# A 31-tap convolution shared by four engines: its TensorE part two dense tiles later, and the taps dealt out anew

## The chip, the cores and the metric

The kernel runs on one core of a Trainium2 chip. The metric is the device time of one execution in microseconds. Three runs of the kernel before took 1447.33, 1449.21 and 1451.06 us; their median is 1449.21 us.

## The reference, cut to what matters

A small transformer of three layers on one sequence of 512 tokens with 1024 features, all in fp32. The third layer's mixer is a conformer convolution: a projection to twice the width, a gate, a depthwise causal convolution over 31 tokens, a layer norm, SiLU, and a projection back.

```
def conformer_conv(x, w_in, b_in, conv_w, conv_b, ln_g, ln_b, w_out, b_out):
    a, g = jnp.split(x @ w_in + b_in, 2, axis=-1)
    h = a * jax.nn.sigmoid(g)
    h = lax.conv_general_dilated(
        h, conv_w[:, None, :].astype(h.dtype), window_strides=(1,),
        padding=[(CONV_KERNEL - 1, 0)],
        dimension_numbers=("NWC", "WIO", "NWC"),
        feature_group_count=D_MODEL) + conv_b
    h = jax.nn.silu(layer_norm(h, ln_g, ln_b))
    return h @ w_out + b_out
...
            y = conformer_conv(h, a_w_in[j], a_b_in[j], a_conv_w[j], a_conv_b[j],
                               a_ln_g[j], a_ln_b[j], a_w_out[j], a_b_out[j])
...
        x = x + y
        x = x + squared_relu_mlp(rms_norm_2(x, mlp_norm[i]), mlp_w1[i], mlp_w2[i])
```

The other two layers (a pooling mixer and a windowed attention, each with a gated feed-forward part) are not touched by the change.

## The kernel before

Features lie on the partitions, tokens along the free dimension, so that an activation of 1024 x 512 is eight chunks of 128x512. Every weight matrix is cut into units of 128 output features (128x1024 weights). A unit passes through four slots: SyncE loads it into `raw`, ScalarE copies it into the fp32r high part `whi` (`split_hi`, line 1027), and somebody makes the low part `wlo`, which is `raw` minus `whi`. TensorE then runs a `chain`: eight tiles of three matmuls (high by high, high by low, low by high, lines 637 to 639), 24 matmuls of 128x512 into one of four banks `acc`.

The convolution stage is the phase `ain`: 16 units, two per chunk c, one for the value and one for its gate. I call the two chains of a chunk its dense tile. Per chunk c, these things happen.

- VectorE evicts both banks (`evict`, line 1799), ScalarE takes the sigmoid of one (`sigmoid`, line 1322), and VectorE multiplies them into `hc` (`gated`, line 1809), a ring of three buffers that also holds 30 zero columns in front.
- The 31 taps of the chunk are shared. TensorE takes the first `PE_TAPS[c]`: SyncE copies shifted windows of `hc` into `shifted` (`shift_hc`, one DMA for each of `SHIFTS[c]` groups of partitions, line 505), VectorE builds small diagonal matrices (`diagonals`, line 1771), and `convolve(c)` runs `ROUNDS[c]` rounds of `SHIFTS[c]` small matmuls side by side (line 914). A round covers as many taps as there are shifts.
- The next `POOL_TAPS[c]` are products made by ScalarE (`products`, line 1300, a ring `tapped` of nine buffers) and added up by GpSimd into `prod` (line 623).
- The rest are VectorE's own taps (`own_tap`, lines 1747 and 1750), each of which adds into a PSUM bank and waits for the one before. TensorE's sets add into the same bank and wait until the chunk's own taps are done. The last `LATE_TAPS[c]` (`late_tap`, line 1760) come after TensorE's sets, and VectorE alternates them with the next chunk's own taps.
- `collect(c)` (line 1793) adds the bank and `prod` into `hv`; for the last chunk, whose own taps lie in another bank, there is an addition more (line 1788). ScalarE squares it (`square`, line 1317) and TensorE sums `hv` and its square over the features (`statistics`, line 937) for the layer norm.

The order on TensorE is: the dense tile of chunk c, `convolve(c-1)`, `statistics(c-3)`. `convolve(5)` is held back until the dense tile of chunk 7 is done, and what is left of the sets and the statistics comes behind it. After that the layer norm and the next projection (`aout`) start.

The low parts of units 6 to 19 (16 and above belong to `aout`) are not VectorE's: `LOW_AT` names, for each, after which addition of GpSimd's chain it is dealt with. Those in `POOL_LOW` are subtracted by GpSimd (line 611). For the others ScalarE writes the negative of `whi` into `wlo` (`negate_high`, line 1309) and GpSimd issues a DMA that adds the weights from HBM onto it (line 605). Their order on ScalarE is written out by hand: the second split of iteration c waits until the dense tile of chunk c+1 is done, since it needs the slot.

SyncE's queue is in order as well: load of unit 2c+6, `shift_hc(c)`, load of unit 2c+7.

Of the kernel before, what the change touches and what calls it, by code (L numbers as in the profile page):

```python
# [30 lines left out]
T = 512  # L31
# [11 lines left out]
PE_TAPS = (6, 6, 8, 8, 12, 12, 20, 14)  # L43
SHIFTS = (2, 2, 4, 4, 4, 4, 4, 2)
# [6 lines left out]
GATE_AT = 8  # L51
STATS_AFTER = 2
COLLECT_AT = 3
R1_CHUNKS = (3, 4, 5, 6)
R1_AT = 3
# [12 lines left out]
POOL_LOW = (6, 7, 8, 9)  # L68
# [109 lines left out]
def build(nc, xT, vec_in, cst_in, w_in, out):  # L178
# [3 lines left out]
    with ExitStack() as ctx:  # L182
# [3 lines left out]
        def sem(name):  # L186
            return ctx.enter_context(nc.semaphore(name))
# [133 lines left out]
        late_steps = sem("late_steps")  # L321
# [21 lines left out]
        def v(name, e=0):  # L343
            return col(vec, VEC[name] + e)
# [4 lines left out]
        def own_taps(c):  # L349
            return range(PE_TAPS[c] + POOL_TAPS[c], TAPS - LATE_TAPS[c])  # L350

# [282 lines left out]
        def _(pe):  # L634
# [383 lines left out]
        def _(act):  # L1018
# [314 lines left out]
            for c in range(C):  # L1333
                act.wait_ge(hc_ready, c + 2)
                products(c, range(4 if c == C - 1 else 2))
                if 2 <= c < C - 1:
                    square(c - 2)
                if c == C - 1:
                    square(c - 2)
                if c + 1 == C - 1:  # L1340
                    products(c, range(2, GATE_PRODUCTS))
                    sigmoid(c + 1)
                    products(c, range(GATE_PRODUCTS, POOL_TAPS[c]))
                else:
                    products(c, range(4 if c == C - 1 else 2, POOL_TAPS[c]))
                if c < C - 2:
                    e = 2 * (c + AHEAD) - (c == 0)
                    split_hi(p.unit, 0, e)
                    sigmoid(c + 1)
                    if e in ADDED:  # L1350
                        negate_high(e)
                    for e in range(2 * (c + AHEAD) + (c > 0), min(2 * (c + AHEAD) + 2, 2 * C + 1)):
                        split_hi(p.unit, 0, e)
                        if e in ADDED:
                            negate_high(e)
                if c == C - 2:
                    split_hi(p.unit, 0, 17)
                    negate_high(17)
            square(C - 2)
            split_hi(p.unit, 0, 18)  # L1360
            negate_high(18)
            nc.scalar.activation(eps[:, 4:5], eps[:, 0:1], ACT.Sqrt)
# [20 lines left out]
        def _(dve):  # L1383
# [353 lines left out]
            def late_taps(c):  # L1737
                return range(TAPS - LATE_TAPS[c], TAPS)

# [12 lines left out]

            def late_tap(c, n, k):

                x, w, at = hc[:, c % HC, k:k + T], v("conv_w", c * TAPS + k), bank[6 + c % 2][:]
                if n == 0:
                    dve.wait_ge(conv_done, c + 1)
                else:
                    dve.wait_ge(late_steps, sum(LATE_TAPS[:c]) + n)
                V.scalar_tensor_tensor(at, x, w, at, op0=ALU.mult, op1=ALU.add).then_inc(late_steps, 1)  # L1760
# [21 lines left out]
            def collect(c):  # L1782

                part = prod[:, c % 2, :]
                dve.wait_ge(tapped_steps, sum(POOL_TAPS[:c + 1]) - c - 1)
                if c == APART:
                    dve.wait_ge(tap_steps, sum(len(own_taps(j)) for j in range(c + 1)))
                    V.tensor_tensor(hv[:, c, :], part, hv[:, c, :], ALU.add).then_inc(own_added, 1)
                    part = hv[:, c, :]
                    dve.wait_ge(own_added, 1)  # L1790
                dve.wait_ge(late_steps, sum(LATE_TAPS[:c + 1]))
                dve.wait_ge(conv_done, c + 1)
                V.tensor_tensor(hv[:, c, :], bank[6 + c % 2][:], part, ALU.add).then_inc(hv_ready, 1)
# [19 lines left out]
            for c in range(C):  # L1813
# [14 lines left out]
                if c < C - 1:  # L1828
                    gated(c)
                if c < C - 1:  # L1830
                    diagonals(c)

                own, late = own_taps(c), late_taps(c - 1) if c else []
                if c == HELD:
                    own = own[:len(own) - HELD_TAPS]
                if c == HELD + 1:
                    held = own_taps(HELD)
                    for n in range(len(held) - HELD_TAPS, len(held)):
                        own_tap(HELD, n, held[n])
                    evict(C - 1, 0)  # L1840
                rounds = max(len(own), LATE_START[c] + len(late))
                issued = [min(n, len(own)) + min(max(n - LATE_START[c], 0), len(late)) for n in range(rounds)]
                split_at = [next((n for n in range(rounds) if issued[n] >= m), rounds - 1) for m in (1, 5)]
                gate_at = next((n for n in range(rounds) if issued[n] >= GATE_AT), rounds - 1)
                for n in range(rounds):
                    for j in range(2):
                        if n == split_at[j] and c < C - 1 and (c or j) and 2 * c + j + AHEAD not in OTHER_LOW:
                            split_lo(p.unit, 0, 2 * c + j + AHEAD)
                    if n == gate_at and c < C - 2:
                        evict(c + 1, 0)  # L1850
                    if n == min(R1_AT, rounds - 1) and c in R1_CHUNKS:
                        invert_residual(R1_CHUNKS.index(c))
                    if n == COLLECT_AT and c == C - 1:
                        collect(C - 2)
                    if n < len(own):
                        own_tap(c, n, own[n])
                    if 0 <= n - LATE_START[c] < len(late):
                        late_tap(c - 1, n - LATE_START[c], late[n - LATE_START[c]])
# [3 lines left out]
                if 0 < c < C - 1:  # L1862
                    collect(c - 1)
# [135 lines left out]
```

## Time and profile before

| | |
|---|---|
| median of three runs | 1449.21 us |
| the profiled execution | 1448.2 us, of which the span is 1446.4 us |
| busy share: TensorE, VectorE, ScalarE, GpSimd | 99%, 63%, 42%, 16% |
| mean granted TensorE clock | 0.996 |
| convolution stage: first tile's inputs to last addition into `hv` | about 921 to 1042 us |
| DMA over the span | 144.95 MB, mean 100 GB/s |

Times in the rows below are microseconds from the span's start. PE is TensorE, PEld its weight loads, DVE VectorE, ACT ScalarE, POOL GpSimd, SP SyncE. A line of the order in time gives the start, the length from the first start to the last end of the merged instructions, engine, line, operation, what is written from what, and the number; what stands in brackets is idle time before it and what ended that. An fp32 matmul leaves two records, so six matmuls count as x12.

### The profile page before, as it was taken

What the parts mean: (1) busy time and instruction counts of PE and PEld (TensorE: products, weight loads), DVE (VectorE), ACT (ScalarE), POOL (GpSimd) and SP (SyncE); (2) the same over time, 40 slices, a digit from 0 to 9 for tenths busy, and PEclk for the clock granted to TensorE, in tenths of its full rate; (3) what the DMA queues carried; (4) which work ended last, traced back from release to release, by engine and by line L of the source; (5) the groups of instructions that cost most, each with busy time, mean ns of one, the idle gap of its engine ahead of it and who ended that gap; (6) DMA issues with size and microseconds to landing.
All of it is one profiled execution on the core that took longest, in us unless ns stands there. A gap on an engine that the chain in (4) does not pass through costs nothing. (4 is left out here: it accounts for less than half of the span.)

```text
span 1446.4 us, 19981 instructions
## 1 busy us (share of the span) xinstructions
PE 1431.5 (99%) x6878; PEld 1168.8 (81%) x6878; DVE 916.0 (63%) x1324; ACT 614.1 (42%) x914; POOL 226.5 (16%) x172
## 2 busy tenths in 40 slices
PE   8999999999999999999999999899999999999999
PEld 7788888888887898888888888667588888888887
DVE  7877773573655667767754756889888653544532
ACT  5544442342546665444422424667664321222210
POOL 7100000000302231000000003599711000000000
PEclk9999999999999999999999999999999999999999
DMA  5233233233431012332332232249813332332321
GB/s 191 88 102 102 89 101 115 74 101 91 122 102 60 30 60 88 102 102 87 101 117 73 98 101 89 90 111 214 217 45 102 116 102 88 101 102 88 102 95 51
DMA packets 49756, 144.95 MB, mean 100 GB/s; under 512 B 10016, under 2 KB 10784, under 8 KB 49696
## 3 DMA queue, kind: packets, MB, share of 16 engines
q1 hardware_dynamic: 47408, 137.34, 29.7%
q0 software_dynamic: 1440, 5.24, 2.0%
q10 hardware_dynamic: 848, 1.59, 0.3%
q8 instruction: 35, 0.57, 0.2%
q14 instruction: 25, 0.20, 0.0%
HBM read 135.14 MB, written 2.10 MB: 95 GB/s over the span
## 5 line engine op out<-in xcount | busy, mean ns | idle before, releaser
L637 PE MATMUL bank<-xh,whi 128*128 128x512 f32 x1184 | 464.8, 393 | 0.2
L639 PE MATMUL bank<-xh,wlo 128*128 128x512 f32 x1184 | 460.9, 389 | 0.0
L638 PE MATMUL bank<-xl,whi 128*128 128x512 f32 x1184 | 460.8, 389 | 0.0
L1027 ACT ACTIVATE whi<-raw 128x1024 fp32r<-128x1024 f32 x244 | 255.7, 1050 | 245.7 <-PE bank L639 239.0
L1392 DVE TENSOR_TENSOR wlo<-raw,whi 128x1024 fp32r<-128x1024 f32 x230 | 288.7, 1255 | 41.7 <-ACT whi L1027 33.6
L637 PEld LDWEIGHTS bank<-xh,whi 128*128 128x128 f32 x1184 | 222.2, 188 | 54.7 <-issue 6.0
L639 PEld LDWEIGHTS bank<-xh,wlo 128*128 128x128 f32 x1184 | 222.2, 188 | 46.7
L638 PEld LDWEIGHTS bank<-xl,whi 128*128 128x128 f32 x1184 | 222.3, 188 | 46.4 <-issue 1.0
L637 PE MATMUL bank<-ahi,whi 128*128 128x512 f32 x608 | 236.5, 389 | 0.0
L638 PE MATMUL bank<-alo,whi 128*128 128x512 f32 x608 | 236.5, 389 | 0.0
L639 PE MATMUL bank<-ahi,wlo 128*128 128x512 f32 x608 | 236.5, 389 | 0.0
L1413 DVE TENSOR_TENSOR res<-bank,res 128x512 f32 (+1 forms) x80 | 55.3, 691 | 200.9 <-PE bank L639 200.9
L582 POOL TENSOR_TENSOR ssum<-ssum,sq 128x512 f32<-128x512 f32 x32 | 48.7, 1521 | 719.8 <-ACT sq L1047 387.3
L1467 DVE SCALAR_TENSOR_TENSOR tmp<-u,vec,tmp 128x512 f32<-128x512 f32 x176 | 124.0, 747 | 29.6 <-ACT tmp L1089 29.3
L638 PEld LDWEIGHTS bank<-alo,whi 128*128 128x128 f32 x608 | 114.1, 188 | 23.8
L637 PEld LDWEIGHTS bank<-ahi,whi 128*128 128x128 f32 x608 | 114.1, 188 | 23.6
L639 PEld LDWEIGHTS bank<-ahi,wlo 128*128 128x128 f32 x608 | 114.1, 188 | 23.6
L1089 ACT ACTIVATE tmp<-u,vec 128x512 f32<-128x512 f32 x88 | 71.5, 814 | 121.6 <-DVE u L1460 121.5
L1460 DVE TENSOR_TENSOR u<-bank,rinv 128x512 f32<-128x512 f32 x88 | 59.5, 686 | 64.0 <-PE bank L639 64.0
L623 POOL TENSOR_TENSOR prod<-prod,tapped 128x512 f32<-128x512 f32 x56 | 78.6, 1404 | 6.5 <-ACT tapped L1300 0.4
L1111 ACT ACTIVATE ahi<-tmp 128x512 f32 (+1 forms) x32 | 20.2, 632 | 121.8 <-DVE tmp L1493 121.8
L1093 ACT ACTIVATE gate<-tmp 128x512 f32<-128x512 f32 x44 | 27.9, 633 | 98.4 <-DVE tmp L1467 98.4
(196 smaller groups left out, 1313.2 us busy)
## 6 DMA issues: line engine op xcount, KB each, us to landing
raw<-w_ffn_up SPq DMA_DIRECT2D x88, 512.0 KB, 3.3
raw<-w_ffn_down SPq DMA_DIRECT2D x32, 512.0 KB, 3.3
raw<-w_mlp_up SPq DMA_DIRECT2D x32, 512.0 KB, 3.3
raw<-w_mlp_down SPq DMA_DIRECT2D x32, 512.0 KB, 3.3
raw<-w_ain SPq DMA_DIRECT2D x16, 512.0 KB, 3.6
raw<-w_ffn_down SPq DMA_DIRECT2D x16, 384.0 KB, 3.1
raw<-w_qkv SPq DMA_DIRECT2D x12, 512.0 KB, 3.3
raw<-w_wo SPq DMA_DIRECT2D x8, 512.0 KB, 3.4
```

Of the source, the lines that this page charges most:

```text
L582: nc.gpsimd.tensor_tensor(ssum[:, which, :], ssum[:, which, :], x, ALU.add)\
L623: nc.gpsimd.tensor_tensor(prod[:, c % 2, :], a, tapped[:, (made + k) % PARTS, :], ALU.add)\
L637: nc.tensor.matmul(out_, hi, mh, start=first, stop=False)
L638: nc.tensor.matmul(out_, hi, ml, start=False, stop=False)
L639: return nc.tensor.matmul(out_, lo, mh, start=False, stop=last)
L1027: nc.scalar.activation(whi[:, s, 0:tiles * P], raw[:, s, 0:tiles * P], ACT.Copy)\
L1089: nc.scalar.activation(tmp[:, k, :], u[:, k, 2:2 + T], ACT.Identity, scale=col(vec, par + 2), bias=col(vec, par + 3))\
L1093: nc.scalar.activation(gate[:, b, :], tmp[:, 2 * b + 1, :], ACT.Silu)\
L1392: V.tensor_tensor(wlo[:, s, 0:tiles * P], raw[:, s, 0:tiles * P], whi[:, s, 0:tiles * P].bitcast(F32), ALU.subtract).then_inc(lo_done, 1)
L1413: V.tensor_tensor(row(res, c), acc[k][:], row(res, c), ALU.add).then_inc(acc_free, 1)
L1460: V.tensor_tensor(u[:, k, 2:2 + T], acc[k][:], rinv[:], ALU.mult).then_inc(acc_free, 1)
L1467: V.scalar_tensor_tensor(tmp[:, k, :], u[:, k, shift:shift + T], col(vec, par + 4 * j + shift), tmp[:, k, :], op0=ALU.mult, op1=ALU.add).t ...
```

## The change

- Every chunk's sets come two dense tiles later: TensorE's order is now the dense tile of chunk c, `convolve(c-2)`, `statistics(c-3)`, without a held chunk.
- All chunks but the last use sets of four shifts. `PE_TAPS` rises from 86 to 98 in all, `POOL_TAPS` falls from 72 to 58, VectorE's taps rise from 90 to 92. There are no late taps.
- VectorE's own taps of chunk c are split over two iterations: `OWN_AT_ONCE[c]` of them in iteration c, the others in iteration c+1, followed by the eviction of the next tile's first bank (`EVICT_AT`), `collect(c-2)` and the diagonals.
- Low parts 8 and 9 go from GpSimd's subtraction to the negation and the accumulating DMA, and the places of all of them are new. ScalarE's order is rewritten: `square(c-3)` comes first in iteration c, sigmoid and first split come between the products.

```diff
-PE_TAPS = (6, 6, 8, 8, 12, 12, 20, 14)
-SHIFTS = (2, 2, 4, 4, 4, 4, 4, 2)
+PE_TAPS = (12, 8, 8, 12, 12, 12, 20, 14)
+SHIFTS = (4, 4, 4, 4, 4, 4, 4, 2)
...
-STATS_AFTER = 2
-COLLECT_AT = 3
+STATS_AFTER = 3
+COLLECT_AT = 8
...
-POOL_TAPS = (11, 10, 10, 9, 9, 9, 8, 6)
-LATE_TAPS = (2, 8, 10, 12, 9, 0, 0, 0)
-HELD = C - 3
-HELD_TAPS = 7
-LATE_START = (2, 2, 2, 0, 0, 0, 0, 0)
+POOL_TAPS = (10, 9, 8, 8, 7, 7, 5, 4)
+OWN_AT_ONCE = (3, 4, 4, 2, 5, 7, 6)
+EVICT_AT = (3, 0, 0, 0, 0, 2, 1)
 PARTS = 9
-GATE_PRODUCTS = 6
+GATE_PRODUCTS = 5
 HC = 3
-LOW_AT = {6: (0, 7), 7: (0, 9), 8: (1, 5), 9: (1, 7), 10: (2, 5), 11: (2, 7), 12: (3, 5), 13: (3, 7), 14: (4, 5), 15: (4, 7), 16: (5, 6), 17: (7, 1), 18: (7, 3),
-          19: (7, 5)}
+LOW_AT = {6: (0, 6), 7: (0, 9), 8: (1, 1), 9: (1, 3), 10: (1, 6), 11: (2, 1), 12: (2, 5), 13: (3, 1), 14: (3, 5), 15: (4, 1),
+          16: (5, 3), 17: (6, 3), 18: (7, 3), 19: (7, 3)}
-POOL_LOW = (6, 7, 8, 9)
+POOL_LOW = (6, 7)
...
-                if 1 <= c <= HELD:
-                    convolve(c - 1)
-                if c == C - 1:
-                    convolve(HELD)
+                if c >= 2:
+                    convolve(c - 2)
                 if c >= 3:
                     statistics(c - 3)
...
             for c in range(C):
+                if c >= 3:
+                    square(c - 3)
                 act.wait_ge(hc_ready, c + 2)
...
+                products(c, range(2 if c == 0 else 0, min(GATE_PRODUCTS, POOL_TAPS[c])))
+                if c < C - 1:
                     sigmoid(c + 1)
...
+                if 1 <= c < C - 2:
+                    split_hi(p.unit, 0, 2 * (c + AHEAD))
+                    if 2 * (c + AHEAD) in ADDED:
+                        negate_high(2 * (c + AHEAD))
+                products(c, range(GATE_PRODUCTS, POOL_TAPS[c]))
+                if c == 0:
+                    split_hi(p.unit, 0, 2 * AHEAD)
+                if c < C - 3:
+                    split_hi(p.unit, 0, 2 * (c + AHEAD) + 1)
+                    if 2 * (c + AHEAD) + 1 in ADDED:
+                        negate_high(2 * (c + AHEAD) + 1)
...
+                gated(c)
+                if c == 0:
+                    split_lo(p.unit, 0, AHEAD + 1)
+                else:
+                    last = own_taps(c - 1)
+                    for n in range(OWN_AT_ONCE[c - 1], len(last)):
+                        own_tap(c - 1, n, last[n])
+                    if c == 1:
+                        diagonals(0)
+                    if EVICT_AT[c] == 0:
+                        evict(c + 1, 0)
+                    if c >= 2:
+                        collect(c - 2)
                     diagonals(c)
...
+                for n in range(OWN_AT_ONCE[c]):
+                    if n and n == EVICT_AT[c]:
                         evict(c + 1, 0)
+                    if c == 0 and n == 2:
+                        split_lo(p.unit, 0, AHEAD + 2)
+                        evict(1, 0)
+                    own_tap(c, n, own[n])
+                if c in R1_CHUNKS:
+                    invert_residual(R1_CHUNKS.index(c))
                 if c == C - 2:
                     gated(C - 1)
                     diagonals(C - 1)
```

## Rows read from the trace of the kernel before

**Rows 1.** The page's busy time and share of the span, with the instructions.
```profile
PE 1431.5 (99%) x6878; PEld 1168.8 (81%) x6878; DVE 916.0 (63%) x1324; ACT 614.1 (42%) x914; POOL 226.5 (16%) x172
```

**Rows 2.** Two stretches of the stage: length, busy by engine, granted clock, DMA, GB/s.
```profile
946.33:960.16 13.83, 13.83 (x62) 9.70 (x60) 9.63 (x14) 6.34 (x9) 13.26 (x9) 1.00 0.23 77
...
987.57:1001.81 14.24, 14.24 (x84) 9.87 (x81) 13.70 (x20) 10.12 (x15) 13.41 (x11) 1.00 0.98 234
```

**Rows 3.** TensorE's order in time at the end of the second dense tile.
```profile
941.01 5.39 PE L914 MATMUL bank<-shifted,dg 128*64 128x512 f32 x12 [5.94 <-DVE bank L1750]
946.33 0.50 PE L637 MATMUL bank<-xh,whi 128*128 128x512 f32 x1
```

**Rows 4.** Stretches as in rows 2, over the hole and behind it.
```profile
935.00:941.00 6.00, 0.07 (x1) 0.02 (x1) 5.82 (x9) 5.00 (x7) 5.43 (x5) 0.87 0.26 89
941.00:945.00 4.00, 3.99 (x10) 1.38 (x12) 3.86 (x4) 2.65 (x5) 4.00 (x3) 0.50 0.31 65
```

**Rows 5.** TensorE's order in time: sets, statistics, the next dense tile.
```profile
957.44 2.80 PE L914 MATMUL bank<-shifted,dg 128*64 128x512 f32 x12
...
971.29 1.92 PE L914 MATMUL bank<-shifted,dg 128*32 128x512 f32 x16
973.03 0.39 PE L937 MATMUL bank<-hv,ones 128*32 128x256 f32 x2
...
973.57 0.50 PE L637 MATMUL bank<-xh,whi 128*128 128x512 f32 x1
...
985.28 1.93 PE L914 MATMUL bank<-shifted,dg 128*32 128x512 f32 x16 [0.52 <-DMA shifted<-hc]
...
1024.58 2.78 PE L914 MATMUL bank<-shifted,dg 128*32 128x512 f32 x24
```

**Rows 6.** The chain that ended last, in the stage's tail: start, length.
```profile
1039.17 1.28 POOL prod L623
...
1041.20 0.70 DVE hv L1793
```

**Rows 7.** VectorE's order in time: diagonals, eviction, alternating taps, taps in a row.
```profile
929.47 0.56 DVE L1771 TENSOR_TENSOR dg<-pair_id,pair_w 128x384 f32<-128x384 f32 x1
...
940.77 0.69 DVE L1799 TENSOR_TENSOR bank<-bank,rinv 128x512 f32<-128x512 f32 x1
...
942.35 2.16 DVE L1771 TENSOR_TENSOR dg<-pair_id,pair_w 128x384 f32<-128x384 f32 x1
...
948.75 0.75 DVE L1750 SCALAR_TENSOR_TENSOR bank<-hc,vec,bank 128x512 f32<-128x512 f32 x1
949.41 0.75 DVE L1760 SCALAR_TENSOR_TENSOR bank<-hc,vec,bank 128x512 f32<-128x512 f32 x1
...
1032.88 5.50 DVE L1750 SCALAR_TENSOR_TENSOR bank<-hc,vec,bank 128x512 f32<-128x512 f32 x7
```

**Rows 8.** ScalarE's order in time: a split, its negation, two products.
```profile
986.70 1.06 ACT L1027 ACTIVATE whi<-raw 128x1024 fp32r<-128x1024 f32 x1
987.78 1.06 ACT L1309 ACTIVATE wlo<-whi 128x1024 fp32r<-128x1024 f32 x1
988.75 1.42 ACT L1300 ACTIVATE tapped<-hc,vec 128x512 f32<-128x512 f32 x2
```

**Rows 9.** GpSimd's order in time: four additions, an accumulating DMA, an addition.
```profile
952.89 5.59 POOL L623 TENSOR_TENSOR prod<-prod,tapped 128x512 f32<-128x512 f32 x4
...
1006.89 0.87 POOL L605 DMA_DIRECT2D wlo<-w_ain  x1
1007.50 1.60 POOL L623 TENSOR_TENSOR prod<-prod,tapped 128x512 f32<-128x512 f32 x1
```

**Rows 10.** Weight loads, median us to landing (from 973, from 987); ScalarE behind one.
```profile
raw<-w_ain SPq DMA_DIRECT2D x2, 512.0 KB, 10.6
...
raw<-w_ain SPq DMA_DIRECT2D x1, 512.0 KB, 12.6
...
1003.68 1.07 ACT L1027 ACTIVATE whi<-raw 128x1024 fp32r<-128x1024 f32 x1 [4.17 <-DMA raw<-w_ain]
```

More of the change, by code:

```diff
@@ L50 @@
 QUADRANT = P // 4
-GATE_AT = 8
-STATS_AFTER = 2
-COLLECT_AT = 3
+STATS_AFTER = 3
+COLLECT_AT = 8
 R1_CHUNKS = (3, 4, 5, 6)
-R1_AT = 3
 DIAGS = 2
-POOL_TAPS = (11, 10, 10, 9, 9, 9, 8, 6)
-LATE_TAPS = (2, 8, 10, 12, 9, 0, 0, 0)
-HELD = C - 3
-HELD_TAPS = 7
-LATE_START = (2, 2, 2, 0, 0, 0, 0, 0)
+POOL_TAPS = (10, 9, 8, 8, 7, 7, 5, 4)
+OWN_AT_ONCE = (3, 4, 4, 2, 5, 7, 6)
+EVICT_AT = (3, 0, 0, 0, 0, 2, 1)
 PARTS = 9
-GATE_PRODUCTS = 6
+GATE_PRODUCTS = 5
 HC = 3
-LOW_AT = {6: (0, 7), 7: (0, 9), 8: (1, 5), 9: (1, 7), 10: (2, 5), 11: (2, 7), 12: (3, 5), 13: (3, 7), 14: (4, 5), 15: (4, 7), 16: (5, 6), 17: (7, 1), 18: (7, 3),
-          19: (7, 5)}
+LOW_AT = {6: (0, 6), 7: (0, 9), 8: (1, 1), 9: (1, 3), 10: (1, 6), 11: (2, 1), 12: (2, 5), 13: (3, 1), 14: (3, 5), 15: (4, 1),
+          16: (5, 3), 17: (6, 3), 18: (7, 3), 19: (7, 3)}
 OTHER_LOW = tuple(LOW_AT)
-POOL_LOW = (6, 7, 8, 9)
+POOL_LOW = (6, 7)
 ADDED = tuple(e for e in LOW_AT if e not in POOL_LOW)
@@ L320, in build @@
         tap_steps = sem("tap_steps")
-        late_steps = sem("late_steps")
         own_added = sem("own_added")
@@ L349, in own_taps @@
         def own_taps(c):
-            return range(PE_TAPS[c] + POOL_TAPS[c], TAPS - LATE_TAPS[c])
+            return range(PE_TAPS[c] + POOL_TAPS[c], TAPS)
         def o_at(t, s):
@@ L1333, in _ @@
             for c in range(C):
+                if c >= 3:
+                    square(c - 3)
                 act.wait_ge(hc_ready, c + 2)
[L1335 to L1341, printed above, removed]
-                    sigmoid(c + 1)
[L1343 to L1355, printed above, removed]
+                if c == 0:
+                    products(c, range(2))
+                    split_hi(p.unit, 0, AHEAD + 2)
+                products(c, range(2 if c == 0 else 0, min(GATE_PRODUCTS, POOL_TAPS[c])))
+                if c < C - 1:
+                    sigmoid(c + 1)
+                if 1 <= c < C - 2:
[9 more added lines that the diff above has]
+                        negate_high(2 * (c + AHEAD) + 1)
                 if c == C - 2:
@@ L1358, in _ @@
                     negate_high(17)
-            square(C - 2)
+            square(C - 3)
             split_hi(p.unit, 0, 18)
             negate_high(18)
+            square(C - 2)
             nc.scalar.activation(eps[:, 4:5], eps[:, 0:1], ACT.Sqrt)
@@ L1735, in _ @@
             V.memset(hc[:, :, 0:TAPS - 1], 0.0).then_inc(hc_ready, 1)
-            def late_taps(c):
-                return range(TAPS - LATE_TAPS[c], TAPS)
             def own_tap(c, n, k):
@@ L1751, in own_tap @@
                                        op0=ALU.mult, op1=ALU.add).then_inc(tap_steps, 1)
[L1753 to L1760, printed above, removed]
             def diagonals(c):
@@ L1790, in collect @@
                     dve.wait_ge(own_added, 1)
-                dve.wait_ge(late_steps, sum(LATE_TAPS[:c + 1]))
                 dve.wait_ge(conv_done, c + 1)
@@ L1827, in _ @@
                     evict(0, 0)
-                if c < C - 1:
-                    gated(c)
-                if c < C - 1:
-                    diagonals(c)
[L1833 to L1849, printed above, removed]
-                        evict(c + 1, 0)
[L1851 to L1858, printed above, removed]
+                own = own_taps(c)
@@ new lines, in _ @@
+                if c == C - 1:
+                    collect(C - 3)
+                    for n, k in enumerate(own):
+                        if n == COLLECT_AT:
+                            collect(C - 2)
+                        own_tap(c, n, k)
+                    continue
+                gated(c)
+                if c == 0:
+                    split_lo(p.unit, 0, AHEAD + 1)
[9 more added lines that the diff above has]
+                        collect(c - 2)
+                    diagonals(c)
@@ L1861, in _ @@
                     diagonals(C - 1)
-                if 0 < c < C - 1:
-                    collect(c - 1)
             mean, mean_sq, var, safe, std = (rms[:, e * NBLK:(e + 1) * NBLK] for e in range(5))
```

## The prediction

> **What bounds the kernel now.** The page comes first: TensorE is busy for 99% of the span [rows 1]. So a microsecond counts only if TensorE waits less or more. The stretches of the convolution stage come next [rows 2]: between its holes TensorE is full, VectorE works 9.6 to 13.7 us of each tile's 14, and the DMA share climbs to 0.98. The order in time on TensorE shows the one large hole [rows 3]: after units 2 and 3 it stands until 941.01, for VectorE's last own tap of chunk 0. The granted clock over it and behind it [rows 4] is 0.87, then 0.50, which is the 1.2 GHz level: (1 - 0.87) x 6.0 / 0.5 = 1.6 us of the hole were already slow, so the clock fell about 4.4 us after TensorE stopped. The sets of chunk 0 then took 5.32 us (941.01 to 946.33 [rows 3]), where chunk 1's same three rounds took 2.72 (a stretch of 13.83 from 946.33 less 11.11 of dense work [rows 2, 3, 5]). From 946 the tiles follow each other, apart from 0.52 us for a shifted transfer in front of chunk 3's sets [rows 5], until the last dense unit ends at 1024.58 [rows 5]. I call that moment E. In the tail GpSimd's last sum ends at 1040.45 and VectorE's last addition into hv starts at 1041.20 [rows 6], 16.6 us after E.
>
> **The change, part by part.** First the durations.
> - TensorE: a tile of two dense units is 11.11 us (946.33 to 957.44 [rows 3, 5]); a round of sets 0.91 with two shifts (2.72 / 3, above) and 0.87 with four (971.29 to 973.03, two rounds [rows 5]); statistics 0.54 (973.03 to 973.57).
> - VectorE: taps in a row on one accumulator start every 0.79 ((5.50 - 0.75) / 6 [rows 7]); alternating between two accumulators they start every 0.66 (948.75, 949.41 [rows 7]). `gated`, an eviction and hc, takes 1.58 (940.77 to the diagonals at 942.35), counted as 1.5; a bare eviction or collect is 0.61 of that, as its 0.69 overlaps the next. The diagonals took 0.56 to 2.16 [rows 7], whatever their size; I take 1.3 to 1.7.
> - ScalarE: a split 1.08 to its negation, a negation 0.97 to the next product, two products 1.42, so 0.7 for one [rows 8]; a square on the same 128x512 at no more than a product, 0.6. GpSimd: 1.43 per addition ((5.59 - 1.30) / 3); an accumulating transfer holds the queue 0.61 and its next addition takes 1.60 instead of 1.30, so 0.9 [rows 9].
>
> *Sets.* Before E both kernels run chunks 0 to 4: 3+3+2+2+3 = 13 rounds, then 3+2+2+3+3 = 13. Twelve taps more cost TensorE nothing; six rounds at 0.91 become 0.87: -0.2. A shifted window of four pieces instead of two for chunks 0 and 1 is SP time and 0.5 MB each; the next weight load starts about 3 us later than before, ten microseconds before its split: nothing.
>
> *Two tiles later.* `convolve(0)` now follows units 4 and 5, whose low parts VectorE makes by about 934 (hc(0) ends just before 929.47 [rows 7]; a low part, 1024 elements wide, at twice an eviction's pace at most 1.6, two taps 1.6, a low part 1.6): the hole (-5.9), the slow sets (-2.6) and the wait for chunk 3's transfer (-0.5) go. With -0.2: -9.2.
>
> *VectorE.* It now has 92 taps for 90, all in series. Iteration 2 is gated 1.5, ten taps 7.8 (9 x 0.79 + 0.66), evict 0.6, collect 0.6, diagonals 1.6, four taps 3.0 = 15.1 us; the six iterations from 1 come to 12.7, 15.1, 14.7, 15.5, 15.3 and 12.8 = 86.1, against TensorE's 13.4 to 14.3 per tile. VectorE falls behind, but the sets ask only for taps finished one iteration earlier, so this alone stops nothing before E.
>
> *GpSimd and ScalarE.* GpSimd loses 14 additions (-20 us) and two low parts by subtraction (2 x 2.4), and gains two transfers (2 x 0.9): it no longer sets the tail. Low parts 8 and 9 cost ScalarE a negation each.
>
> *The new wait.* `square(c-3)` now stands at the head of iteration c, behind the second split and negation of iteration c-1, while TensorE asks for its statistics in the same tile c. The chain to it is: evict(c,0) 0.7, sigmoid 0.6, split and negation 2.1, GpSimd's accumulating transfer and the addition behind it 2.3, ScalarE's last product 0.6 (it waits for that addition), split and negation 2.1, square 0.6, and seven hand-overs of under 0.1: 9.4 us. It cannot start before the tile's first unit is done, and TensorE then has 5.55 + 1.74 = 7.3 us: at least 2.1 us of waiting at the two-round tiles, 3 and 4.
>  - At tile 3 VectorE is late too. From evict(1,1) at 935.1: `gated` 1.5, six taps 4.6, diagonals, evict, diagonals 3.6, four taps 3.0, `gated` 1.5, ten taps 7.8: evict(3,0) starts at 957.1, and square(0) ends 9.3 later at 966.4. TensorE is there at 935.03 + 11.11 + 2.61 + 11.11 + 1.74 = 961.6. A wait of 4.9.
>  - Unit 11's split also needs its load, issued behind the four pieces at 953.4. Such loads landed after 10.6 and 12.6 us [rows 10] once accumulating transfers ran beside them; with 10.6 the wait is 5.3.
>  - That passes the 4.4 us after which the clock fell before, so I add the 2.6 us that it cost then.
>  - Tile 4: 2.2. Tile 5 has three rounds and no GpSimd in the chain: split, negation and square 2.8 after the tile against 2.6, and a load landing 0.8 late: 1.1.
>  Together 5.3 + 2.6 + 2.2 + 1.1 = +11.2, and E moves by -9.2 + 11.2 = +2.0.
>
> *Tail.* From E: sets of chunk 5 2.6, diagonals(7) 2.0, collect(5) 0.6, eight taps 6.3, collect(6) 0.7, square 0.7: statistics(6) at E + 13.0, where TensorE stands 1.3 us; two rounds 1.8, sums by token 1.0, last round 0.95, hand-over: the last addition starts at E + 17.3, against 16.6: +0.7.
>
> Sum: +2.7 on the profiled execution's 1448.2 (span 1446.4 and 1.8 around it) = 1450.9. The median of the runs is 1.0 above that execution, so 1451.9.
>
> *A rule against a row.* The rows say that a tap which waits for the one before costs 0.13 us more than one that does not [rows 7]. The Trainium skill, "VectorE: DVE Perf Modes", section "The DRAIN you can't avoid", says that a semaphore between VectorE operations costs nothing extra. By that rule the sum would be about 4 us under before, as in the last rival.
>
> **The rivals.**
> - *Loads land late each time* (slower). The DMA share was 0.98 and ScalarE waited 4.17 us for such a load [rows 2, 10]. If the loads of units 11, 13 and 15 land after 12.6, each of tiles 3 and 5 waits 2 us longer: +4.0, and 1455.9; diagonals at 2.16 every time add up to 1.2. It decides from about 11.5 us on. Against it: two transfers spread over longer tiles.
> - *Square comes in time, VectorE sets the pace* (faster). If the trace's chain is shorter than I make it, no wait is left; then gated(7) starts at 935.1 + 86.1 = 1021.2 and the last addition 16.0 later, 1037.2 against 1041.20: -4.0, 1445.2, and 1443.5 with diagonals at the 0.56 of the first one. Against it: the 2.1 us floor needs none of the uncertain prices.
> - *Taps start every 0.66 even in series* (the rule above). The twenty taps in front of evict(3,0) save 2.6, the wait at tile 3 is 2.3 to 3.3, the clock stays up, the tail is 1 us shorter: -4.0, 1445.2. Against it: the series of seven in rows 7, 0.79 apart.
> - *The change does nothing that counts*: its own waits just fill the hole; that lies inside my forecast.
>
> **How the numbers follow.** A run can tell about 0.3%, 4.35 us, from no change: 1444.9 to 1453.6. Forecast 0.55 (0.46 inside, 0.09 slower, since its own range is 1448.4, with the clock kept and loads in time, to 1455); late loads 0.20 (0.18 slower, 0.02 inside); VectorE's pace 0.15 (0.08 faster, 0.07 inside); quick taps 0.10 (0.03 faster, 0.07 inside). In sum faster 0.11, same 0.62, slower 0.27. Range 1445 to 1457.
>
> **What the changed profile would show.** No hole at 935; TensorE's wait for VectorE's tap replaced by waits of the 128x256 statistics for sq: about 5, 2 and 1 us at tiles 3, 4, 5, and half clock behind the first. E near 1026.6, GpSimd idle in the tail, taps in series 0.79 apart. If statistics wait under 1 us the whole middle of the sum is wrong; if half clock does not show, 2.6 comes off; if a dense chain waits for a low part, I have missed a transfer.

## The result and the profile after

The changed kernel took 1452.52 us in the median of 16 runs (1450.36 to 1455.74), the kernel before 1448.11 in 16 runs beside it (1446.71 to 1451.06): a ratio of 1.0031, 95% interval 1.0023 to 1.0039, so 4.4 us slower. The forecast was 1451.9 with a range of 1445 to 1457, and +2.7 as the difference. A second measurement gave 1.0036 (1.0024 to 1.0048).

The profiled execution took 1450.36 us. Its page, busy time per engine:

```profile
span 1448.6 us, 19996 instructions
PE 1432.2 (99%) x6902; PEld 1170.2 (81%) x6902; DVE 917.5 (63%) x1326; ACT 608.3 (42%) x902; POOL 203.6 (14%) x158
```

Only GpSimd's time moved much, 226.5 to 203.6 us [rows 1], and the end did not follow it. TensorE's waits in the convolution stage, each line with the sum in us, the count and the longest:

```profile
PE bank L932 <- ACT sq L1310: 9.0, 4, 5.9
PE bank L951 <- DVE hv L1772: 0.2, 1, 0.2
```

The wait for VectorE's tap [rows 3] and the one for the shifted transfer [rows 5] are gone. In their place TensorE waits four times for ScalarE's squares: three times at tiles 3 to 5 and once, 0.69 us, in the tail. (The second line is the short wait at the end of the stage, which the kernel before has too.) Its order in time shows where:

```profile
945.08 2.78 PE L909 MATMUL bank<-shifted,dg 128*32 128x512 f32 x24
...
966.74 0.64 PE L932 MATMUL bank<-hv,ones 128*32 128x256 f32 x2 [5.90 <-ACT sq L1310]
...
967.75 0.80 PE L632 MATMUL bank<-xh,whi 128*128 128x512 f32 x1
...
984.20 0.64 PE L932 MATMUL bank<-hv,ones 128*32 128x256 f32 x2 [2.18 <-ACT sq L1310]
...
985.21 0.80 PE L632 MATMUL bank<-xh,whi 128*128 128x512 f32 x1
...
1000.37 0.41 PE L932 MATMUL bank<-hv,ones 128*32 128x256 f32 x2 [0.20 <-ACT sq L1310]
...
1026.32 2.78 PE L909 MATMUL bank<-shifted,dg 128*32 128x512 f32 x24
```

TensorE now goes from unit 3 into units 4 and 5 without a stop, and the sets of chunk 0 follow at 945.08 in 2.78 us and not in 5.39 [rows 3]. Then the statistics of tiles 3, 4 and 5 wait 5.90, 2.18 and 0.20 us. The last row is E, the end of the last dense unit. Stretches of the same kernel (length, busy time of each engine, granted clock, DMA share, GB/s):

```profile
961.00:963.00 2.00, 0.00 (x0) 0.00 (x0) 1.87 (x3) 0.72 (x1) 1.86 (x2) 1.00 1.00 272
964.00:965.00 1.00, 0.00 (x0) 0.00 (x0) 0.96 (x2) 0.99 (x1) 0.76 (x1) 0.50 1.06 262
...
970.00:971.00 1.00, 1.00 (x5) 0.78 (x4) 0.94 (x2) 0.72 (x1) 0.87 (x1) 0.79 0.97 202
...
984.00:985.00 1.00, 0.81 (x8) 0.23 (x8) 0.93 (x3) 1.00 (x3) 1.00 (x2) 0.54 0.95 175
...
987.00:988.00 1.00, 1.00 (x5) 0.73 (x4) 0.96 (x2) 0.52 (x1) 0.86 (x2) 0.76 0.76 121
```

The granted clock goes to its 1.2 GHz level twice: within the wait at tile 3 and, which the forecast did not have, at the end of the wait at tile 4. Each spell is paid for in the statistics (1.01 us from 966.74 to 967.75 and from 984.20 to 985.21, against 0.54 [rows 5]) and at the head of the dense tile. ScalarE's order in time ahead of the first wait:

```profile
956.89 0.73 ACT L1315 ACTIVATE gate<-tmp,vec 128x512 f32<-128x512 f32 x1 [0.18 <-DVE tmp L1778]
957.52 1.04 ACT L1020 ACTIVATE whi<-raw 128x1024 fp32r<-128x1024 f32 x1
958.60 1.06 ACT L1302 ACTIVATE wlo<-whi 128x1024 fp32r<-128x1024 f32 x1
959.56 1.32 ACT L1293 ACTIVATE tapped<-hc,vec 128x512 f32<-128x512 f32 x2
962.17 0.72 ACT L1293 ACTIVATE tapped<-hc,vec 128x512 f32<-128x512 f32 x1 [1.28 <-POOL prod L618]
963.93 1.06 ACT L1020 ACTIVATE whi<-raw 128x1024 fp32r<-128x1024 f32 x1 [1.04 <-DMA raw<-w_ain]
965.02 1.06 ACT L1302 ACTIVATE wlo<-whi 128x1024 fp32r<-128x1024 f32 x1
965.98 0.61 ACT L1310 ACTIVATE sq<-hv 128x512 f32<-128x512 f32 x1
```

Here is the chain that the forecast set up, link by link: sigmoid, split and negation, a product held by GpSimd, a split held by its load, a negation, the square. VectorE's order in time, for its pace and the tail:

```profile
923.08 3.30 DVE L1804 RECIPROCAL rinv<-rms 128x512 f32<-128x512 f32 x1
...
948.38 7.88 DVE L1739 SCALAR_TENSOR_TENSOR bank<-hc,vec,bank 128x512 f32<-128x512 f32 x10
956.17 0.68 DVE L1778 TENSOR_TENSOR tmp<-bank,rinv 128x512 f32<-128x512 f32 x1
956.77 0.68 DVE L1772 TENSOR_TENSOR hv<-bank,prod 128x512 f32<-128x512 f32 x1
957.37 0.41 DVE L1751 TENSOR_TENSOR dg<-pair_id,pair_w 128x256 f32<-128x256 f32 x1
...
1043.15 0.69 DVE L1772 TENSOR_TENSOR hv<-bank,hv 128x512 f32<-128x512 f32 x1 [0.32 <-PE bank L909]
```

The first row is a mark for lining up the two executions: the same operation started at 923.87 before, so this one runs 0.79 us ahead at the stage's start. With that, E moved by 1026.32 + 0.79 - 1024.58 = +2.5 us, and the last addition into hv by 1043.15 + 0.79 - 1041.20 = +2.7.

### The profile page after: what moved, and what is told of

Its sections match the earlier page's. It is cut to its first block, busy times and chain, and to the rows that moved or that the text cites. A ratio compares the mean times of both kernels' runs of the same rounds, so it can differ in the third digit from the quotient of the medians.

```text
span 1448.6 us, 19996 instructions
## 1 busy us (share of the span) xinstructions
PE 1432.2 (99%) x6902; PEld 1170.2 (81%) x6902; DVE 917.5 (63%) x1326; ACT 608.3 (42%) x902; POOL 203.6 (14%) x158
## 4 chain that ended last, share of the span: by engine, by line
PE 91%; POOL 4%; DVE 1%; issue 1%; DMA 1%; ACT 1%; SPq 0%; ACTq 0%; POOLq 0%; DVEq 0%
PE bank L632 29%; PE bank L633 28%; PE bank L634 28%; POOL prod L618 2%; PE bank L783 1%; PE bank L811 1%; POOL res L567 1%; PE bank L796 1%; POOL ssum L577 1%; PE bank L909 1%; DMA res<-xT 1%; PE bank L997 0%; PE bank L998 0%; DMA raw<-w_ain 0%; PE bank L1001 0%
## 5 line engine op out<-in xcount | busy, mean ns | idle before, releaser
L1739 DVE SCALAR_TENSOR_TENSOR bank<-hc,vec,bank 128x512 f32<-128x512 f32 x83 | 62.7, 755 | 2.8
```

What stands on the lines that cost most here:

```text
L1739: V.scalar_tensor_tensor(hv[:, c, :] if c == APART and n == len(own_taps(c)) - 1 else at, x, w, at, op0=ALU.mult, op1=ALU.add).then_inc(ta ...
```

## The experiments

All ran in three sessions of four, each with 14 to 29 runs of the kernel before beside them (medians 1448.35, 1448.00 and 1448.64 us). Since these medians differ by 0.6 us, I compare each kernel by its difference to the kernel before of its own session. "Kernel 2" is the kernel of experiment 2, and so on. The diffs are against the changed kernel unless another is named.

**1. The changed kernel once more.** No edit.

> The changed kernel once more, unchanged, as the measure for its neighbours on the same chip. All theories: about 1.003 of the kernel before. Its profile is of another execution, so it also tells how much the wait in front of the statistics of chunk 0 (5.90 us in the first profile) and the half clock behind it differ from one execution to the next.

Measured: 1453.26 us (1451.42 to 1455.24), ratio 1.0036 (1.0024 to 1.0048), +4.9. The wait at tile 3 was 8.06 us in this execution. Its rows on TensorE and on ScalarE:

```profile
968.89 0.64 PE L932 MATMUL bank<-hv,ones 128*32 128x256 f32 x2 [8.06 <-ACT sq L1310]
```
```profile
966.09 1.06 ACT L1020 ACTIVATE whi<-raw 128x1024 fp32r<-128x1024 f32 x1 [3.19 <-DMA raw<-w_ain]
```

The split of unit 11 waited 3.19 us for its load, not 1.04, and the whole chain behind it came 2.16 us later. What varies from one execution to the next is the landing of that load, not its issue: SyncE starts on these loads at 952.5 us here and at 952.7 in the first profile, and those issued between 950 and 966 us took a median of 14.2 us here and 11.2 there.

**2. The square earlier.** The square of chunk c-2 directly behind the sigmoid of tile c+1, ahead of the two splits.
```
             for c in range(C):
-                if c >= 3:
-                    square(c - 3)
...
                 if c < C - 1:
                     sigmoid(c + 1)
+                if 2 <= c < C - 1:
+                    square(c - 2)
```

> Only ScalarE's order differs: square(c-2) right behind sigmoid(c+1) in iteration c, before the splits, instead of at the head of the next iteration. Theory 1 (the squares come late, behind the second split and negation): the waits of 5.9, 2.2 and 0.2 us and the 1.7 us of half clock go, the last dense unit of the stage ends 9 to 10 us earlier; VectorE then sets the tail, and 5 to 7 us are left in the whole, so 1446 us, below the kernel before. Theory 2 (VectorE's 92 taps in series set the pace anyway): the waits change their name to VectorE and the time stays within 1.5 us of the changed kernel. Theory 3 (the transfers are late): the splits still wait for loads and a dense unit for its low part, and the time stays.

Measured: 1440.86 us (1440.64 to 1443.55), ratio 0.9956 (0.9942 to 0.9969): -7.5 to the kernel before, some 12 less than the changed kernel. TensorE's waits in the stage and the stretches of tiles 4 to 7:

```profile
PE bank L909 <- DMA shifted<-hc: 1.5, 1, 1.5
PE bank L932 <- ACT sq L1310: 1.2, 2, 1.0
```
```profile
961.00:974.50 13.50, 13.50 (x77) 9.70 (x73) 12.98 (x19) 9.15 (x13) 10.27 (x9) 1.00 1.03 276
974.50:988.00 13.50, 13.50 (x72) 9.65 (x76) 13.02 (x18) 10.80 (x15) 10.98 (x9) 1.00 0.92 196
```

The waits of tiles 3 to 5 and both half-clock spells are gone; TensorE is busy for all of each stretch at full clock. E lies at 1014.03, 12.3 us earlier; the last addition starts at 1033.55, 9.6 earlier; most of the difference is that chunk 7's set now waits 1.51 us for its shifted copies and the statistics ahead of it 0.99 us for their square. ScalarE's split of unit 11 still waited 1.67 us for its load there, and it did no harm: nothing that TensorE needs at once stood behind it.

**3. The statistics later.** The square stays where the change put it; TensorE asks for it a tile later.
```
-                if c >= 3:
-                    statistics(c - 3)
+                if c >= 4:
+                    statistics(c - 4)
             convolve(C - 2)
+            statistics(C - 4)
```

> Only TensorE's order differs: the statistics one dense tile later (statistics(c-4) in tile c), the squares where the change put them. Theory 1: the same gain as with the early square, 5 to 7 us, since nobody asks for the square in its own tile any more, though ScalarE's chain is as long as before. Theory 2 and 3: no gain. If this gains and the early square doesn't (or the other way round), the chain in front of the square is not what I think.

Measured: 1441.32 us (1441.15 to 1442.86), ratio 0.9954 (0.9941 to 0.9968), -7.0. This is the same gain from the other end of the same dependence: what cost time was that square and statistics stood in one tile with two splits between, neither place by itself.

**4. TensorE kept busy in the wait.** 20 matmuls whose results nobody reads, behind the sets of chunk 1.
```
+                if c == 3:
+                    pe.wait_ge(acc_free, p.chain + 5)
+                    for _ in range(20):
+                        nc.tensor.matmul(acc[0][:, 0:P], ones[:], ones[:], start=True, stop=True)
                 if c >= 3:
                     statistics(c - 3)
```

> The changed kernel with 20 small matmuls (128x128 of ones into a bank whose contents are used no more) between the sets of chunk 1 and the statistics of chunk 0, about 4.8 us of work inside the wait of 5.9 us. They compute nothing that is used. Theory 1 with its clock term: the wait stays, the granted clock stays at 1.0 through the fourth dense tile, and 1.5 to 2 us are gained. If the clock cost nothing or is paid elsewhere: no gain, or a loss if the small matmuls last longer than the wait.

Measured: 1452.72 us (1450.26 to 1453.64), ratio 1.0027 (1.0017 to 1.0037), +4.4: no gain. The matmuls ended at 965.8, but the load was late in this execution, the statistics waited another 3.44 us, and the clock fell in that time (1.00 up to 969, 0.68 from 969 to 970, 0.50 behind). So this run does not show what the clock is worth; the next one does.

**5. The same with 28 matmuls.** `range(28)` in place of `range(20)`.

> As the run with a busy wait, with 28 instead of 20 idle-work matmuls (6.6 us) between the sets of chunk 1 and the statistics of chunk 0, so that TensorE is busy to 967.6 and stands still at most 1.3 us where the squares come at 966.7 to 968.9. If the clock fell because TensorE stood still: no half-clock spell at tile 3, statistics 0.64 us and the dense part of tile 4 11.19 us (12.4 in the changed kernel), the wait at tile 4 of 2.2 us and its half-clock spell stay; 0.5 to 1.6 us faster than the changed kernel, the fills costing back up to 0.9 us where the squares were ready before they end. If the clock falls for another reason (work done before the wait), the spell stays and the time is that of the changed kernel, 1452.5, or above.

Measured: 1451.01 us (1447.63 to 1453.07), ratio 1.0012 (1.0003 to 1.0021), +2.4. The stretches over the wait at tile 3, which now stands still for 1.76 us, and behind the one at tile 4 (2.18):

```profile
967.00:968.00 1.00, 0.33 (x3) 0.14 (x2) 0.93 (x3) 0.97 (x2) 0.00 (x0) 1.00 1.01 317
968.00:969.00 1.00, 0.00 (x0) 0.00 (x0) 0.96 (x2) 1.00 (x3) 0.28 (x1) 1.00 1.04 374
969.00:970.00 1.00, 0.91 (x10) 0.49 (x11) 0.96 (x2) 1.00 (x2) 1.00 (x2) 1.00 1.05 385
970.00:971.00 1.00, 1.00 (x6) 0.83 (x5) 0.96 (x2) 0.92 (x3) 0.92 (x1) 1.00 1.17 346
...
987.00:988.00 1.00, 1.00 (x4) 0.74 (x3) 0.93 (x2) 0.48 (x1) 1.00 (x1) 0.50 0.92 144
```

The square came as late as in experiment 1 (968.3), but the clock stayed at full. The dense part of tile 4 took 11.1 us, not the 12.3 to 12.4 of the changed kernel, and the statistics 0.57 instead of 1.01. So the clock falls because TensorE stands still, and the first spell is worth 1.2 + 0.4 = 1.6 us. The spell at tile 4, where nothing was filled in, is still there. The gain of 2.0 to 2.5 us over the changed kernel is that plus what chance gave to the loads.

**6. Low parts 10 and 12 later on GpSimd.**
```
-LOW_AT = {..., 10: (1, 6), 11: (2, 1), 12: (2, 5), ...}
+LOW_AT = {..., 10: (1, 8), 11: (2, 1), 12: (2, 7), ...}
```

> GpSimd forms low parts 10 and 12 two places later in its run of adds (10 before its add 8 of chunk 1, 12 before its add 7 of chunk 2), all else as in the changed kernel. Theory 1 (statistics of a tile wait because ScalarE's squares stand behind a split and a negation): ScalarE's products wait less for GpSimd's buffers ahead of the square for tile 4, so the wait of 2.18 us there falls towards 1.2 us and the half clock behind it shortens; the wait at tile 3 stays where the split waits for the raw load (5.9 to 8.1 us) and falls to about 4.5 us where it does not. Sum: 1 to 2 us faster than the changed kernel, 1450.5 to 1452 where that one takes 1452.5. Theory 2 (VectorE's 92 taps set the pace): nothing, 1452.5. Theory 3 (late raw loads make the wait at tile 3): the wait at tile 3 stays 5.9 to 8.1 us, so at most 1 us.

Measured: 1450.12 us (1448.6 to 1452.25), ratio 1.0016 (1.0007 to 1.0025), +2.1. The wait at tile 4:

```profile
983.61 0.41 PE L932 MATMUL bank<-hv,ones 128*32 128x256 f32 x2 [1.06 <-ACT sq L1310]
```

It halved from 2.18 us as expected, and behind it the clock did not fall: 0.41 us per matmul here, 0.64 in the changed kernel. The wait at tile 3 was 6.7 us in this execution, bound by the load (the split waited 3.24 us), and a wait of 0.78 us stood at tile 5, where the split of unit 15 had waited 1.36 us for its load. The gain over the changed kernel is 2.3 us or more; 1.1 of waiting and 1.6 of half clock would be 2.7.

**7. The load ahead of the shifted copies.**
```
-                shifts = {2 * c + KT - 2: c for c in range(C)}
+                shifts = {2 * c + KT - 1: c for c in range(C)}
```

> SyncE's queue issues the load of slice 2c+7 ahead of the shifted copies of chunk c instead of behind them; all else as in the changed kernel. Theory 3 (the split ahead of the square of tile 0 waits for a raw load that was issued late and lands 11 to 14 us after its issue): loads are issued and land 1 us or more earlier, the wait of the split of 1.04 us (3.19 us in the other execution) goes, and the wait of the statistics at tile 3 falls from 5.9 (8.1) us to about 4.9 us: 1 to 3 us faster than the changed kernel, 1449.5 to 1451.5, and executions spread less. Theory 1 alone (only the place of the square counts, loads are in time in most executions): within 0.5 us of the changed kernel. Against both: if the shifted copies are then late, the four-tap sets wait for them and E moves later.

Measured: 1450.85 us (1447.36 to 1451.98), ratio 1.0014 (1.0005 to 1.0023), +2.9. ScalarE's split of unit 11 no longer waits for anything (963.16, behind its product at 962.54) and the statistics wait 4.74 us instead of 5.90 or 8.06. That is the bare chain; the forecast had it at 4.9 without the load. It is worth 1.5 to 2.0 us over the changed kernel. The executions did not spread less, though (4.6 us), which I had expected.

**8. The four-tap sets alone, in the kernel before.** PE_TAPS and SHIFTS as changed, all else as before. The late taps of chunk 3 were left at 12, so this kernel counts taps 19 and 20 of that chunk twice and does not compute the same function; experiment 9 has each tap once.
```
-PE_TAPS = (6, 6, 8, 8, 12, 12, 20, 14)
-SHIFTS = (2, 2, 4, 4, 4, 4, 4, 2)
+PE_TAPS = (12, 8, 8, 12, 12, 12, 20, 14)
+SHIFTS = (4, 4, 4, 4, 4, 4, 4, 2)
```

> One part of the change alone, in the kernel before: its number of taps on TensorE and the four-tap sets (12, 8, 8, 12 taps with four shifts for chunks 0 to 3), with its old order, its late taps, its GpSimd taps and low parts. The hole of TensorE at 941 us came from VectorE's work of the diagonals and own taps; 6, 2, 0 and 4 taps leave VectorE for TensorE, each set costs TensorE less per tap. Theory A (these parts carry what the change gains, and the late squares of the new order take it away): the hole of 5.9 us shrinks to about 2.5 us, about 3 us faster than the kernel before: 1444 to 1447. Theory B (the gain comes only with the convolution two tiles later): the hole stays at 5 to 6 us and the time at 1448, or above it by the extra sets on TensorE (about 1 us).

Measured: 1450.34 us (1448.81 to 1453.14), ratio 1.0015 (1.0005 to 1.0024), +2.3. The hole shrank to 2.4 us, as theory A said (what is left of it is a wait for a shifted transfer), and the time rose nevertheless: a wait of 5.4 us for a shifted transfer had come up in front of chunk 3's sets. Half clock lay behind both waits: the sets took 4.39 and 4.64 us, against 2.78 at full clock.

**9. The same with 9 late taps of chunk 3**, each tap once.
```
-LATE_TAPS = (2, 8, 10, 12, 9, 0, 0, 0)
+LATE_TAPS = (2, 8, 10, 9, 9, 0, 0, 0)
```

> The kernel before with the changed number of taps on TensorE and four-tap sets alone, now with 9 late taps of chunk 3 instead of 12, so that no tap is counted twice. In the run before it the hole of TensorE at 941 us had shrunk from 5.9 to 2.4 us but a new wait of 5.4 us stood ahead of chunk 3's set at 984.5 us, for shifted copies whose gate had waited for ScalarE behind GpSimd's adds, and the time was 1450.3. If that wait comes from GpSimd's share (10 adds and two low parts in a tile) and not from the two taps counted twice: the wait stays at 4 to 6 us, and the time within 1.5 us of 1450.3 (3 taps fewer on VectorE change little). If the doubled taps made it: the wait falls to under 2 us and the time to 1445 to 1447.

Measured: 1450.06 us (1449.06 to 1451.92), ratio 1.0010 (1.0001 to 1.0019), +1.4. TensorE's waits in the stage, the two sets behind them, then GpSimd's order in time and VectorE's gated value that the transfer carries:

```profile
PE bank L914 <- DMA shifted<-hc: 9.5, 2, 7.2
```
```profile
936.53 2.78 PE L914 MATMUL bank<-shifted,dg 128*32 128x512 f32 x24 [2.31 <-DMA shifted<-hc]
...
984.02 5.35 PE L914 MATMUL bank<-shifted,dg 128*32 128x512 f32 x24 [7.19 <-DMA shifted<-hc]
```
```profile
957.43 2.40 POOL L611 TENSOR_TENSOR wlo<-raw,whi 128x1024 fp32r<-128x1024 f32 x1
959.79 2.73 POOL L623 TENSOR_TENSOR prod<-prod,tapped 128x512 f32<-128x512 f32 x2
962.48 2.39 POOL L611 TENSOR_TENSOR wlo<-raw,whi 128x1024 fp32r<-128x1024 f32 x1
964.83 2.72 POOL L623 TENSOR_TENSOR prod<-prod,tapped 128x512 f32<-128x512 f32 x2
```
```profile
971.15 0.75 DVE L1809 SCALAR_TENSOR_TENSOR hc<-bank,vec,gate 128x512 f32<-128x512 f32 x1 [2.27 <-ACT gate L1322]
```

The wait did not come from the doubled taps. GpSimd is busy for 14.3 of the 15 us from 957 to 972, with two subtractions for low parts and its additions. ScalarE's products wait for it and the sigmoid stands behind them. TensorE reaches chunk 1's sets 7.1 us earlier than in the kernel before (950.35 against 957.44), but the gated value of chunk 3 comes only 1.2 us earlier (971.15 against 972.38), and the shifted transfer lands 7 us too late. In the old order GpSimd was the second bound, directly behind the hole. The clock is the second thing to see here: behind the wait of 7.19 us the sets ran at half clock, but behind the one of 2.31 us they took 2.78 us, which is full clock.

**10. The early square with 8 taps more on VectorE.** Against kernel 2:
```
-PE_TAPS = (12, 8, 8, 12, 12, 12, 20, 14)
+PE_TAPS = (8, 8, 8, 8, 12, 12, 20, 14)
```

> The early square, with 8 taps of chunk 0 and 8 of chunk 3 on TensorE instead of 12 and 12; the 8 taps go to VectorE, which has 100 instead of 92 of them (0.79 us each, 6.3 us in all), and TensorE's sets of chunks 0 and 3 are 0.9 us shorter each. If VectorE has no room left once the statistics wait is gone (busy 12.9 of 13.4 us in a tile): VectorE's gates come up to 6 us later, E and the end with them, 1445 to 1447 against 1440.9 of the early square alone. If TensorE sets the pace and VectorE has slack (two taps fewer on it had moved the end nowhere): within 2 us of 1440.9.

Measured: 1446.66 us (1445.47 to 1448.92), ratio 0.9988 (0.9980 to 0.9997): -2.0 to before, 5.5 more than kernel 2. TensorE's waits in the stage:

```profile
PE bank L909 <- DVE bank L1739: 4.3, 4, 2.0
PE bank L909 <- DMA shifted<-hc: 1.9, 1, 1.9
```

8 taps are 6.3 us of VectorE, and 4.3 come back as waits ahead of sets. Behind two waits, 2.00 us ahead of chunk 3's set and 1.92 ahead of chunk 7's, lie about 3.4 us of half clock each. The second one:

```profile
1030.28 5.35 PE L909 MATMUL bank<-shifted,dg 128*64 128x512 f32 x16 [1.92 <-DMA shifted<-hc]
```

The same set took 3.65 us in kernel 2, behind a wait of 1.51 us. With the squares in time VectorE stands right at the edge, and the four-tap sets, useless alone in the old order, are what keeps it on the right side of it.

**11. Two taps fewer on VectorE.** Against kernel 2, with its order around the evictions and collections shifted by a place:
```
-POOL_TAPS = (10, 9, 8, 8, 7, 7, 5, 4)
-OWN_AT_ONCE = (3, 4, 4, 2, 5, 7, 6)
-EVICT_AT = (3, 0, 0, 0, 0, 2, 1)
+POOL_TAPS = (11, 9, 9, 8, 7, 7, 5, 4)
+OWN_AT_ONCE = (4, 4, 4, 2, 5, 7, 6)
+EVICT_AT = (4, 1, 1, 0, 1, 2, 1)
...
-COLLECT_AT = 8
-GATE_PRODUCTS = 5
+COLLECT_AT = 7
+GATE_PRODUCTS = 4
```

> The early square together with an even load on VectorE: 2 taps more to GpSimd (11 and 9 of chunks 0 and 1, not 10 and 9; chunk 2 gets 9 for 8), 4 at once of chunk 0, evictions one tap later for chunks 1, 2 and 4, chunk 6 collected one tap earlier, 4 gate products. With the early square alone VectorE is busy 12.9 of 13.4 us in each tile and its last add starts at 1033.55 of a span of 1438.9. Theory 1 with VectorE as the next bound: each tap that leaves VectorE in tiles 2 to 5 takes 0.79 us off its run, two taps 1.6 us, and the order of the rest 1 to 1.5 us: 1438 to 1440, so 1 to 3 us under the early square alone (1440.9). If TensorE sets the pace there (its dense tiles of 11.19 us and sets of 2 to 3 us), no change: 1440.9. If GpSimd becomes late, collects wait for it and it is slower than 1440.9.

Measured: 1442.93 us (1442.31 to 1444.39), ratio 0.9964 (0.9950 to 0.9978), -5.1: 2.4 us behind kernel 2, a miss. A statistics wait of 1.08 us came back, and the set of chunk 7 waited 3.43 us for its shifted copies. The trace places the loss in the tail. Chunk 7's copies were issued at the same moment as in kernel 2 (1019.65 and 1019.64) and landed later (medians of 6.0 and 4.5 us), so its set started at 1027.05 and not at 1025.11. The clock fell in that wait and the set ran at half clock almost to its end: its statistics followed 6.3 us after its start, against 3.8. The last addition came at 1038.00 instead of 1033.55. Several things were changed at once, so this run does not say which of them made the copies late; it shows no gain from two taps fewer on VectorE.

**12. Early square and load first together.** Kernel 2 with the edit of 7.

> The early square, with SyncE's load of slice 2c+7 issued ahead of the shifted copies of chunk c. With the square early, no statistics stand behind the split that waits for that load: the earlier load is worth little at tile 3, but splits and low parts of the later tiles are in time more often, and the shifted copies are issued 0.6 to 1.3 us later and share the transfer rings with the load. Within 1 us of the early square alone (1440.9) if loads and copies trade evenly; up to 2 us slower if the sets then wait for their shifted copies (1.5 us waited ahead of chunk 7's set there already).

Measured: 1441.42 us (1440.26 to 1444.99), ratio 0.9951 (0.9938 to 0.9963), -7.2, against -7.5 of kernel 2: no difference. Where no statistics hang on the split, the earlier load buys nothing that these runs can tell. The profiled execution was the slowest of its five (1444.99): there chunk 7's set waited 2.67 us for its copies and ran at half clock, as in experiment 11.

Kernels 2, 3 and 12 are faster than both the kernel before and the changed one; they are not told apart by these runs.

## Why the prediction was right, and where its sum was off

**What went as written.** The hole, the slow sets and the wait for chunk 3's transfer are gone, and GpSimd no longer ends the tail. The new waits stand at the three tiles named, behind the operation named, and half clock lies behind the first. Taps in series start every 0.79 us (7.88 for ten: (7.88 - 0.75) / 9). The evictions and hand-overs follow the chain of the forecast: evict(3,0) was put at 957.1 on the clock of the kernel before and came at 956.17 + 0.79 = 957.0. The waits hang on how the square's place and the statistics' place lie to each other: kernels 2 and 3 take them away by two different edits, one on ScalarE and one on TensorE, and both give back 12 us.

**The terms of the sum**, forecast against measured:
- The wait at tile 3: 5.3; 5.90 in the first profile, 8.06 in the second, 6.7 in kernel 6. The bare chain was right (4.9; 4.74 with the load out of the way). The load's part was mis-sized: 0.4 forecast, from a landing after 10.6 us, and 1.2 to 3.3 measured, with medians of 11.2 and 14.2 us. This was the rival "loads land late", which decides "from about 11.5 us on". At tile 3 it holds in four of the five profiles in which the load stood behind the copies and the square behind the split (kernels 1, 4, 5 and 6: the split waited 3.2 to 3.3 us; the first profile: 1.04); at tile 5 it happened in kernel 6 alone (0.78), and elsewhere 0.20 was waited instead of the 1.1 of the forecast.
- The clock: 2.6, once. Measured 1.2 + 0.5 behind tile 3 and 1.1 + 0.5 behind tile 4, 3.3 together. The forecast took 4.4 us of standing still from the one fall that it had seen [rows 4] as the point from which it is paid, and gave the wait of 2.2 at tile 4 nothing. The same clock fell 2.1 us after TensorE stopped there. That is the step that failed. By luck its error was nearly made up for by each spell being cheaper than the old one: at half clock TensorE lost half of the 2.5 us of dense work in each spell, where behind the old hole all of chunk 0's sets lay in it.
- The wait at tile 4: 2.2; 2.18. Kernel 6 shows that it came through GpSimd's transfer in front of the last product, as the chain had it.
- E: +2.0; +2.5. By terms: -9.2 + 5.90 + 2.18 + 0.20 + 3.3 = +2.4, where -9.2 is the forecast's own figure for what the change takes away; no run measures it by itself.
- The tail: +0.7; 1043.15 - 1026.32 = 16.8 against 16.6, so +0.2. Diagonals(7) took 1.09 us where 2.0 were counted, and TensorE stood 0.69 us for its square where 1.3 were counted.
- The sum: +2.7 for this execution; +2.2 by the spans (1448.6 and 1446.4), +4.4 by the medians. The profiled execution of the change was the fastest of its 16 runs, with the shorter wait at tile 3 of the two profiles. That 1451.9 came so near 1452.52 is partly luck: the median of before, 1449.21 from three runs, was 1.1 above that of sixteen, while the measured difference, +4.4, is 1.7 more than the +2.7 forecast.

**The rivals.** VectorE's pace, if the squares came in time: kernel 2 is that case, and it went to -7.5, not -4.0. From evict(1,1) to `gated` of chunk 7 VectorE took 84.0 us (934.11 to 1018.09) and not 86.1, and from there 15.5 to the last addition and not 16.0; the diagonals of chunks 2 to 6, at 0.41 to 1.20 us instead of 1.3 to 1.7, are most of it. The rest is that the mark of the stage's start lay 1.0 us earlier in that execution. Quick taps in series are refuted by the row of ten. The Trainium skill ("VectorE: DVE Perf Modes", "The DRAIN you can't avoid") has the semaphore cost nothing extra, measured on copies. That does not carry over to these taps, each of which reads the accumulator that the one right before it wrote: they start every 0.79 us, and every 0.66 where two accumulators alternate [rows 7]. The change was not without effect: it took away some 9 us and put 11.6 us of waits and slow clock in their place.

**What was not shown.** Why the copies landed late in kernel 11, and how much of the difference between executions comes from other things than the load of unit 11. That the load lands late because of the accumulating transfers beside it was argued, not tried: the DMA share over 950 to 966 us was 0.98 to 1.00 in the profiles of kernels 1 to 7 and of the changed kernel, and no run took those transfers away. Why the clock falls behind some short stops and not behind others stays open too.

## What to carry to other kernels

When a consumer is moved in time, look at what its producer's engine does between: an operation of 0.6 us placed behind two splits and a wait for a load held up TensorE for 6 to 8 us at one tile and for 2 at the next, and moving that one operation made 12 us. A large change that moves the time little may hold two large terms of opposite sign; take TensorE's waits by name before and after, as a list of a few lines each, and they show it. And count the clock as a possible price of a stop of TensorE even when the stop is only 2 us long.

## What the runs showed of the hardware

- The granted clock fell 2.1 and 2.8 us after TensorE had stopped in the changed kernel's first profile (tiles 4 and 3), 4.9 in kernel 1, 3.6 in kernels 4 and 5, 5.1 in kernel 7. In some cases (kernels 4 and 7 at tile 3, kernel 5 at tile 4, both spells of kernel 10) it fell only after TensorE had started again.
- The length of a short stop does not decide it in these runs. The clock was at half behind the wait of 2.18 us at tile 4 in all five profiles that had it, and behind 1.92 and 2.00 us (kernel 10) and 2.40 us (kernel 8). It stayed up behind 1.06 us (kernel 6), 1.51 (kernel 2), 1.76 (kernel 5) and also 2.31 us (kernel 9). So one observed fall, as in [rows 4], is no bound for the next.
- The raw weight loads, 512 KB each, land after 3.2 us elsewhere in this kernel. Those issued between 950 and 966 us, beside accumulating transfers and shifted copies, landed after medians of 11.2 to 14.2 us (of two or three loads) in the changed kernel and kernels 1 to 7, at a DMA share of 0.98 to 1.00 and a mean of 205 to 230 GB/s.
